# Expert weights laid into the partitions by neighbouring rows, and the tokens gathered in that order

## What is computed

```
# h: 256 tokens x 1024; w_gate, w_up: [32, 1024, 512]; w_down: [32, 512, 1024]
grp = argmax(h @ w_rg + b_rg)                  # 1 of 4 groups
top_val, top_idx = top_k(logits in grp, 2)     # 2 of its 8 experts
gate = softmax(group logits)[grp] * softmax(top_val)
for each expert e, its tokens xb:
    hid = silu(xb @ w_gate[e]) * (xb @ w_up[e])
    out[tokens] += gate * (hid @ w_down[e])
```

## Time and profile before

| | |
|---|---|
| median of 3 runs | 1475.56 us (1472.04 to 1477.86) |
| span of the profiled execution | 1473.6 us |
| PE busy | 1315.1 us, 89% |
| DVE, ACT busy | 745.1 us, 450.9 us |
| DMA | 355.42 MB, 179465 packets, mean 241 GB/s |
| experts, from the first gate and up to the end | 976.8 to 1473.6 us |

### The profile page before, as it was taken

One profiled execution on the slowest core, in us unless ns is written; L12 is line 12 of the kernel. 1 busy time (PEld: TensorE's weight loads), 2 busy tenths in 40 slices (PEclk: granted clock), 3 DMA queues, 4 the chain that ended last, 5 costly groups with the idle time before them and its releaser, 6 DMA issues.

```text
span 1473.6 us, 16820 instructions
## 1 busy us (share of the span) xinstructions
PE 1315.1 (89%) x6278; PEld 903.2 (61%) x6278; DVE 745.1 (51%) x1520; ACT 450.9 (31%) x731; POOL 39.4 (3%) x80
## 2 busy tenths in 40 slices
PE   5979999989977789999887895779999998999995
PEld 4867888876745677888766884654444343344332
DVE  3675555566647669998784998431111111111113
ACT  4424444445443244444442643211001000011001
POOL 0000000000000001221000000000000000000000
PEclk8989999999986699999987998779999999999998
DMA  7345555633530268899551320689999999999993
GB/s 255 116 144 197 174 172 182 207 124 115 177 131 1 86 219 290 304 313 317 211 172 58 115 86 1 261 332 362 336 408 405 404 407 409 409 406 404 407 408 124
DMA packets 179465, 355.42 MB, mean 241 GB/s; under 512 B 7418, under 2 KB 63411, under 8 KB 179410
## 3 DMA queue, kind: packets, MB, share of 16 engines
q1 hardware_dynamic: 172066, 327.96, 60.3%
q0 software_dynamic: 6912, 25.17, 5.0%
q10 hardware_dynamic: 432, 1.57, 0.3%
HBM read 353.63 MB, written 1.05 MB: 241 GB/s over the span
## 4 chain that ended last, share of the span: by engine, by line
PE 62%; DVE 16%; DMA 14%; SPq 4%; ACT 3%; issue 1%; DVEq 0%; ACTq 0%
DMA odd_expert<-in_moe_w_up 13%; PE ps L385 13%; PE ps L387 12%; PE ps L386 12%; PE ps L2345 11%; DVE xn L2001 4%; PE ps L2374 3%; SPq L561 3%; DVE w_lo L359 2%; PE ps L2334 2%; PE ps L2383 1%; DMA dense_weights<-in_ev_w_in 1%; PE ps L1855 1%; SPq L988 1%; DVE ada_acc L1834 1%
## 5 line engine op out<-in xcount | busy, mean ns | idle before, releaser
L359 DVE TENSOR_TENSOR w_lo<-dense_weights,w_hi 128x1024 fp32r<-128x1024 f32 (+1 forms) x228 | 270.6, 1209 | 142.9 <-ACT w_hi L354 142.5
L354 ACT CAST w_hi<-dense_weights 128x1024 fp32r<-128x1024 f32 (+1 forms) x228 | 233.7, 1038 | 277.1 <-PE ps L387 240.9
L385 PE MATMUL ps<-w_hi,xT_lo 128*128 128x512 f32 (+1 forms) x624 | 252.4, 405 | 35.2 <-DVE xT_lo L2036 12.9
L386 PE MATMUL ps<-w_lo,xT_hi 128*128 128x512 f32 (+1 forms) x624 | 246.8, 396 | 0.0
L387 PE MATMUL ps<-w_hi,xT_hi 128*128 128x512 f32 (+1 forms) x624 | 246.8, 395 | 0.0
L385 PEld LDWEIGHTS ps<-w_hi,xT_lo 128*128 128x128 f32 x624 | 121.1, 194 | 64.8 <-issue 19.0
L387 PEld LDWEIGHTS ps<-w_hi,xT_hi 128*128 128x128 f32 x624 | 120.7, 193 | 25.9
L386 PEld LDWEIGHTS ps<-w_lo,xT_hi 128*128 128x128 f32 x624 | 121.2, 194 | 24.6 <-issue 0.5
L2345 PE MATMUL ps<-odd_expert,ge_xT 128*64 128x512 f32 x480 | 108.0, 603 | 15.9 <-DMA odd_expert<-in_moe_w_up 15.9
L2463 DVE COPY ge_y<-ps 128x512 f32<-128x512 f32 x32 | 22.1, 692 | 197.7 <-PE ps L2374 197.7
L2468 DVE SCALAR_TENSOR_TENSOR ge_a<-ge_th,ps 128x256 f32<-128x256 f32 x32 | 13.5, 421 | 206.3 <-ACT ge_th L2420 206.3
(11 more groups left out here) (376 smaller groups left out, 1747.0 us busy)
## 6 DMA issues: line engine op xcount, KB each, us to landing
dense_weights<-in_moe_w_gate SPq DMA_DIRECT2D x16, 2048.0 KB, 16.6
dense_weights<-in_moe_w_up SPq DMA_DIRECT2D x16, 2048.0 KB, 21.5
dense_weights<-in_moe_w_down SPq DMA_DIRECT2D x16, 2048.0 KB, 14.1
odd_expert<-in_moe_w_gate SPq DMA_DIRECT2D x15, 2048.0 KB, 18.4
odd_expert<-in_moe_w_up SPq DMA_DIRECT2D x15, 2048.0 KB, 18.9
odd_expert<-in_moe_w_down SPq DMA_DIRECT2D x15, 2048.0 KB, 18.2
ada_w<-in_ada_w POOLq DMA_DIRECT2D x48, 512.0 KB, 5.1
dense_weights<-in_w_gate SPq DMA_DIRECT2D x22, 1024.0 KB, 7.5
```

Of the source, the lines that this page charges most:

```text
L354: act.copy(split_view(w_hi, name, i, j), piece(name, i, j)).then_inc(hi_ready, 1)
L359: dve.tensor_tensor(split_view(w_lo, name, i, j), piece(name, i, j), split_view(w_hi, name, i, j).bitcast(F32), ALU.subtract).then_inc(pie ...
L385: pe.matmul(out, left[1], right[0], start=start, stop=False)
L386: pe.matmul(out, left[0], right[1], start=False, stop=False)
```

## The change

Gate and up: partition p now takes the eight neighbouring features 8p to 8p + 7, which is one run of 16 KB in HBM, and chunk q holds the features 8p + q. Gate and up lie one behind the other in the tile (`two k f`) rather than by turns, so the run is whole on the SBUF side too. Down: each half of 256 hidden rows gives two neighbouring rows to a partition, 8 KB runs, two per partition.

For the products to stay the same, the tokens are permuted: ACT writes `xn` so that columns 128q to 128q + 127 are the features 8p + q (it reads `ps` at every eighth word), and `ge_hid` is transposed from every second column. The `AllTokens` branch makes its own `hnT` from the permuted `xn` with 16 transposes and 4 copies. The early expert's down rows take three DMAs and not two, and its other loads get runs of 8, 4 and 2 KB.

The core of the diff:

```diff
@@ -238,7 +238,7 @@
         with scope() as experts:
-            early_rows = experts("early_rows", [P, KC // 2, 2, EXPERT_HID])
+            early_rows = experts("early_rows", [P, 2, KC // 2, EXPERT_HID])
...
+        xn_rows = xn[:].rearrange("p t (q c r) -> p t q c r", q=KC, c=KC)
...
         def gate_up_of(e):
-            return expert_tiles[e % 2][:, 0:KC * 2 * EXPERT_HID].rearrange("p (k two f) -> p k two f", k=KC, two=2)
+            return expert_tiles[e % 2][:, 0:KC * 2 * EXPERT_HID].rearrange("p (two k f) -> p two k f", k=KC, two=2)
...
         def gate_up_chunks(flat):
-            return flat.rearrange("p (k two f) -> p k two f", two=2, f=EXPERT_HID)
+            return flat.rearrange("p (two k f) -> p two k f", two=2, f=EXPERT_HID)
...
             view, k = early_gate_up[k] if e == EARLY else (gate_up_of(e), k)
-            return view[:, k]
+            return view[:, :, k]
...
-            g = a["moe_w_gate_2"][0].rearrange("e (k p) f -> p e k f", p=P)
-            u = a["moe_w_up_2"][0].rearrange("e (k p) f -> p e k f", p=P)
-            d = a["moe_w_down_2"][0].rearrange("e (c p) d -> p e c d", p=P)
+            g = a["moe_w_gate_2"][0].rearrange("e (p k) f -> p e k f", p=P)
+            u = a["moe_w_up_2"][0].rearrange("e (p k) f -> p e k f", p=P)
+            d = a["moe_w_down_2"][0].rearrange("e (h p c) d -> p e h c d", p=P, c=2)
 
             def gate_up(e, it):
                 for side, w in enumerate((g, u)):
-                    sp.dma_start(gate_up_of(e)[:, :, side, :], w[:, per_round(e, it, 2)]).then_inc(gu_landed[e % 2], 16)
+                    sp.dma_start(gate_up_of(e)[:, side], w[:, per_round(e, it, 2)]).then_inc(gu_landed[e % 2], 16)
 
             def down(e, it):
-                sp.dma_start(down_of(e), d[:, per_round(e, it, 2)]).then_inc(down_landed[e % 2], 16)
+                sp.dma_start(down_of(e).rearrange("p (h c) d -> p h c d", c=2), d[:, per_round(e, it, 2)]).then_inc(down_landed[e % 2], 16)
...
-            sp.dma_start(early_down_rows[:], d[:, EARLY, 0:EARLY_DOWN_ROWS]).then_inc(early_landed, 16)
-            sp.dma_start(g_bc[:, 0], d[:, EARLY, EARLY_DOWN_ROWS]).then_inc(early_landed, 16)
+            sp.dma_start(early_down_rows[:, 0:2], d[:, EARLY, 0]).then_inc(early_landed, 16)
+            sp.dma_start(early_down_rows[:, 2], d[:, EARLY, 1, 0]).then_inc(early_landed, 16)
+            sp.dma_start(g_bc[:, 0], d[:, EARLY, 1, 1]).then_inc(early_landed, 16)
...
                     act.wait_ge(self.turned, b + 1)
-                    act.copy(xn[:, b // 2, (b % 2) * 512:(b % 2 + 1) * 512], ps[:, 4 + b, :])
+                    act.copy(xn_rows[:, b // 2, :, (b % 2) * 4:(b % 2 + 1) * 4, :],
+                             ps[:, 4 + b, :].rearrange("p (c r q) -> p q c r", c=4, q=KC))
...
+                for b in range(4):
+                    for c in (2 * b, 2 * b + 1):
+                        for t in range(T):
+                            last = pe.transpose(ps[:, b, (c % 2) * S + t * P:(c % 2) * S + (t + 1) * P], xn[:, t, c * P:(c + 1) * P], ident[:])
+                    last.then_inc(self.x_turned, 1)
+                pe.wait_ge(self.xT, 4)
                 gate_up(0, None, 0)
...
-                            last = pe.transpose(ps[:, 0, n:n + P], ge_hid[:, e, c * P:(c + 1) * P], ident[:])
+                            last = pe.transpose(ps[:, 0, n:n + P], ge_hid[:, e].rearrange("p (j c) -> p c j", c=2)[:, c], ident[:])
```

More of the change, by code:

```diff
@@ L61 @@
 EARLY_DOWN_ROWS = EXPERT_HID // P - 1
-EARLY_DMAS = 2 * 4 + 2
+EARLY_DMAS = 2 * 4 + 3
 class Part:
@@ L428, in build @@
             view = gate_up_chunks(memory)
-            early_gate_up += [(view, k) for k in range(view.shape[1])]
+            early_gate_up += [(view, k) for k in range(view.shape[2])]
         first_places = 2
@@ L570, in early_expert @@
                     for side, w in enumerate((g, u)):
-                        sp.dma_start(view[:, :, side, :], w[:, EARLY, first:first + view.shape[1]]).then_inc(early_landed, 16)
+                        sp.dma_start(view[:, side], w[:, EARLY, first:first + view.shape[2]]).then_inc(early_landed, 16)
             sp.wait_ge(ple_used, 4)
@@ L2163, in __init__ @@
                 self.blocks = MOE_BLOCKS
+                self.x_turned, self.xT = other.share_turned, other.xT
                 self.gate_up = other.gathered
@@ L2209, in turn @@
                             last = pe.transpose(ps[:, 2, c * S + t * P:c * S + (t + 1) * P],
-                                                all_hid[:, n % 2, t, c * P:(c + 1) * P], ident[:])
+                                                all_hid[:, n % 2, t].rearrange("p (j c) -> p c j", c=2)[:, c], ident[:])
                     last.then_inc(self.turned, 1)
@@ L2252, in step @@
                     tanh(n, it, 1)
+                for b in range(4):
+                    act.wait_ge(self.x_turned, b + 1)
+                    act.copy(hnT[:, 2 * b:2 * b + 2, :], ps[:, b, :].rearrange("p (c s) -> p c s", c=2)).then_inc(self.xT, 1)
                 tanh(0, None, 0)
```

## The result

The changed kernel takes 1455.8 us, the median of four runs (1451.17 to 1459.89); the kernel before beside it takes 1474.98 (1472.04 to 1477.86). The ratio is 0.9872, with a 95% interval of 0.9848 to 0.9897: 19 us, 1.3%, faster. The profiled execution took 1452.09 us with a span of 1450.4, 23.2 less than the span before.

The account below looks back on a forecast made before the run. The weight stream was taken as the bound, PE right behind. Span 1473.6 - 18.2 + 0 + 0 = 1455.4; the median, 2.0 above, 1457.4, with half a us of waits 1458. Range 1454 to 1478.

Parts of the forecast that it names:

- The bound: Experts' stage: the weight stream bounds at 30.91 us a pair, 2.0 above PE's 28.91, costing 18.2 us in all.
- A: Weight loads: long runs are slower because of the place read in memory; 386 GB/s gives 1494 us; chance 0.13.
- B: Weight loads: run length doesn't set the rate, or hardware cuts runs to 2 KB; period 30.9, 1475.6 us; chance 0.13.
- The line through 2 KB and 4 KB: DMA cost per engine: 5.2 ns a run plus 36.5 ns a KB, extended to 435 GB/s at 16 KB.
- The period: Weight stream after the change: 29.0 us a pair, 19.3 for gate and up plus 9.7 for down.
- The threshold: Experts' stage: the whole 18.2 us come back below 29.26 us a pair, with a stream lead of 3.8 us.
- The signs named for "right": Experts' profile: groups 28.9 us apart, waits under 3 us, some 430 GB/s then idle, clock 1.00, four transposes 0.44 us.
- D, between: Weight loads: 424 GB/s for all or the even expert's handicap stays; 1461 to 1462 us; counted within the forecast's 0.66.
- The clock: PE behind waits: the granted clock, 0.94 on the mean, returns to 1.00 when the waits go; within the 18.2 us.
- rival C: PE's hidden-row transposes: the strided weight load doubles, 9.0 us over 64, giving 1467 us; chance 0.08.
- ACT's copies: Four copies to `xn` at stride eight: 0.59 us each, cost 0; upper bound 1.88 each, about 3 us on the path.
- SP: Early expert's down rows: one DMA more at 1.2 us, hidden by 16 us of cover, costs nothing.

Follow-up runs that it names:

- light form of before: Kernel before the change, but pairs 1 to 14 give back only the first 128 tokens, which relieves PE: 1467.12 us, one run.
- cut kernel: Changed kernel, but gate and up interleaved in the SBUF tile, so each consecutive 16 KB lands as 2 KB pieces: 1469.02 us, ratio 0.9969.
- down alone: Changed kernel with gate and up (2 KB runs, interleaved tile) and ACT's copies as before, only down changed: 1473.21 us, ratio 0.999.
- gate and up alone: Changed kernel with down rows, hidden transposes and early down rows as before; gate and up keep 16 KB runs: 1455.21 us, ratio 0.9878.
- exchanged sources: Kernel before, but from expert 6 on each tile of a pair loads the other expert's gate and up weights: 1475.19 us, one run.
- light 8 KB: Changed kernel, pairs 1 to 14 giving back only the first 128 tokens, gate and up in runs of 8 KB: 1456.81 us, one run.
- light after: Changed kernel, but pairs 1 to 14 give back only the first 128 tokens: 1455.64 us, one run.
- light 4 KB: Changed kernel, pairs 1 to 14 giving back only the first 128 tokens, gate and up in runs of 4 KB: 1454.84 us, one run.
- odd expert first: Kernel before with pairs 1 to 14 giving back only 128 tokens, odd expert's gate and up issued ahead of the even one's: 1604.67 us, one run.

## Why the prediction was right, and where it was off

**The bound** was read rightly. PE behind the stream by 30.91 - 28.91 a pair is what the change took away, and in the light form of before PE's saved work went into waits and into the lower clock behind them.

**Length, not place (rivals A and B).** The line through 2 KB and 4 KB was the step on which most hung. It was said that its ends differ only in run length, but they differ in tensor too, as B says. What was extrapolated with it to 16 KB held all the same: 430 GB/s in the full stretch, not 386 (A) and not 407 (B). The cut kernel shows that place has no part in it: consecutive 16 KB read as 2 KB pieces are back at 409. The 6% of the even tile, the one thing that spoke for A, isn't the memory that is read either: it stayed when the sources were exchanged.

**The period was the mis-sized term.** 29.0 us were put, 29.28 measured. The cost of a run was near (5.2 ns put, 4.6 measured without the slow stretch); the part that goes with bytes was 1% too cheap: 36.5 ns a KB makes 28.7 us for a pair's 786 KB per engine, where the runs give 28.94. The line took the faster tile's 2 KB rate and the 4 KB rate of five windows of 2 us, and its two points lie close together beside the distance to 16 KB. The estimate from the Trainium skill, page "DMA: Bandwidth & Descriptors", 29.15 us, was the nearer one. Its section "Where 436 GB/s comes from", with 435 GB/s, agrees with the 435 at which the line of the periods ends. Its section "Why small descriptors are slow (HBM only)" has about 3 cycles a packet, and 32 bytes of descriptor metadata beside them, which the prediction left out. At 36.8 ns a KB the 3 cycles of 32 bytes are 3.5 ns, and with the metadata it is 4.7, an estimate from that page. The 4.6 ns of the runs agree with it; the stretch with 5 ns more isn't in it.

**The threshold.** The whole gain was said to need a period under 29.26; 29.28 is just beyond. By the formula 11 x (29.28 - 28.91) - 3.8 = 0.3 us of waits remain; 1.4 were lost. PE's own pair had become 28.94 and the stream's lead was shorter than the 3.8 us taken over from before: 11 x (29.28 - 28.94) - 1.4 leaves 2.3. Why it was shorter isn't shown. The signs named for "right" came but for three: from 1266.94 on the groups are 29.28 apart and not 28.9, the transposes take 0.47 us, and no windows of idle came, since the stream never has time to spare. "D, between" was nearer the truth in its mechanism than the forecast, at about a third of its price.

**The clock** came back with the waits, as said: 1.00 in the windows that had 0.94.

**The strided weight load (rival C)** came half true. Of the two signs that were named, a load over 200 ns is there (206); 0.6 us for the four isn't, and nor is the price. The matmul that a load precedes took the time anyway: four transposes take 0.47 us, not 0.44, and 64 of them cost about 0.5 us, not 9.0. The mistake in C was to take the time of a load as time of PE's path, where most of it overlaps the matmul before. That two reads in a 16-byte line go at full speed (the Trainium skill, page "SBUF — State Buffer", section "Door 1: The DMA port swizzle") isn't what this weight load shows: it has 206 ns in the changed kernel as in that with down alone.

**ACT's copies** with every eighth word of PSUM are what they were, as the earlier trace rows, with 0.27 idle between; the bound of 1.88 us a copy, and the 3 us that it would have cost, were far off.

```profile
957.90 0.58 ACT L2092 COPY xn<-ps 128x512 f32<-128x512 f32 x1 [0.27 <-PE ps L2078]
```

**SP.** The early expert's down rows held it longer than the 1.2 us an instruction that the earlier trace rows gave, and stayed hidden: it was done at 953.7 and had nothing to issue before 979.11.

```profile
940.12 2.24 SPq L585 DMA_DIRECT2D early_down_rows<-in_moe_w_down  x1
942.40 7.57 SPq L586 DMA_DIRECT2D early_down_rows<-in_moe_w_down  x1
950.01 3.67 SPq L587 DMA_DIRECT2D g_bc<-in_moe_w_down  x1
979.11 0.33 SPq L563 DMA_DIRECT2D dense_weights<-in_moe_w_gate  x1
```

**The sum.** The experts' stage gave back 18.4 us against the 18.2 predicted, and part of that agreement is luck. What the steps foresaw is 18.2, less 1.4 of waits that stay, less 0.5 for the transposes: 16.3, and 16.4 were found up to the pair before the last. Of the rest 1.7 us are the last down group at full clock, which no step had. The median, 1455.8, is 2.2 below the forecast of 1458, and the four runs fall at 1451 to 1452 and at 1459 to 1460, more than that apart. Over the profiled executions of all these kernels the start of the first expert scatters by 8.7 us in early code that hardly differs between them, so neither this 2.2 nor a difference of a few us between two kernels here can be read without that start.

**What is next.** PE's own 28.94 us a pair and the stream's floor of 28.94 are now the same: longer runs or fewer bytes alone can give back no more than the 1.4 us still lost, since then PE is the bound. Taking work from PE helps little while the stream needs 29.28: of 25 us it gave 4.9. Only both together would give more; that wasn't tried. No form here beats the change; that with gate and up alone is as fast and simpler.

## What to carry to other kernels

When DMA engines are busy throughout and a consumer waits once in each round, take the period of the rounds and fit it against the number of runs per engine: here 28.9 us for the bytes and some 5 ns for each run. The form of before (320 runs) lay 6.8% above its bytes, that of after (64 runs) 1.2%. Look at the packets' records as well: a slow stretch can pass for a steeper line. Cap what is to be gained by the next bound before costing it (PE's 28.91 leaves 2.0 us of the stream's 30.91, and would at any rate of the DMA), and cost a stride in a weight load by the time of its group of instructions, not by the load's own. Compare two versions from the first point at which they differ: here 4.8 of 23.2 us had nothing to do with the change.

## What the runs showed of the hardware

- In a full stream a packet costs its engine 4.6 ns beside its bytes, the same from 2 to 16 KB. In one stretch of each pair it is up to 5 ns more (records of 89 ns for 84 at 2 KB, 164 for 159 at 4 KB). With 2 KB runs that stretch is the later part of the even expert's load (387 GB/s for 410), whichever expert is read and whichever comes first, also with TensorE idle. Its cause is open.
- Pieces that are consecutive in memory but not in the tile are packets of their own: 171,417 of them against 114,841.
- A float32 weight load of 128x128 with a stride of two words takes 206 ns, with plain columns 140, at full clock; behind matmuls that costs 0.03 us in four.
- SP can stand in a DMA instruction for long. It was 8.09 us in a load of 1024 runs, and it is 0.34 in one of 128:

```profile
1296.26 0.34 SPq L563 DMA_DIRECT2D dense_weights<-in_moe_w_up  x1
```

  The load's own runs aren't the reason: at 942.40 (above) it stood 7.57 us in a load of 128 runs, behind eleven loads issued within 15.4 us. That it waits for room in its queue fits both and isn't shown.
- The last group of 32 matmuls, with no transfer beside it, took 8.78 us in the profiles of before, of down alone, of the exchanged sources and (8.75) of light 8 KB, and 7.09 in those of after, gate and up alone, cut, light before, light after, light 4 KB and odd expert first. What decides it isn't settled.
